# Order of work in three attention stages of a two-block transformer kernel: where weight halves, turns and tiles stand

## The chip, the cores and the metric

The kernel runs on one core of one Trainium2 chip, in one launch. The metric is the device time in microseconds (us), the median over runs. In the kernel and below, PE is TensorE, ACT is ScalarE, DVE is VectorE, POOL is GpSimd and SP is SyncE, which here only issues DMAs.

## The reference, cut to what matters

The input is one sequence of 512 tokens with 1024 features, all in fp32. A first block has two layers; each mixes three branches (latent attention with 4 heads, gated linear attention, retention) and then runs a wide gated feed-forward net. A second block has three more branches: dilated windows, grouped queries, and an attention over 256 memory rows.

```python
# first block, twice
z = rmsnorm(x, attn_norm[l]) @ w_in[l]
y_a = head_rmsnorm(mla_branch(...), mla_out_norm[l])          # causal, 4 heads, 4 blocks of 128 queries
y_b = gla_branch(...)
y_c = retention_branch(...)                                   # head norm, times silu(gate)
x = x + jnp.concatenate([y_a, y_b, y_c], axis=-1) @ w_out[l]
x = x + (jax.nn.silu(causal_dwconv(a)) * bv) @ ffn_w_down[l]
# second block
qb_, kb_ = normed and turned queries (8 heads) and keys (2 heads)
ob = softmax(qb_ @ kb_.T) @ vb_                               # the grouped-query branch
kvm = rms_norm(mem, g_mem) @ w_mem_kv                         # 256 memory rows
om = softmax(mq @ km.T) @ vm
merged = gates[0] * ((oa*silu(ga)) @ w_br_a) + gates[1] * ((ob*silu(gb)) @ w_br_b) + gates[2] * (...)
x = x + rms_norm(merged @ w_out, g_post)
```

## The kernel before, in words

**Products in halves.** Every fp32 matrix is held as a high part and a low part (`w_hi`, `w_lo`; `h_hi`, `h_lo`), and a product is three matmuls: high by high, low by high, high by low (lines 863 to 865, and 1285 to 1287 for the layers' output projection). A "tile" is 128 output rows by 512 tokens and takes 24 matmuls where the inner size is 1024, 12 where it is 512.

**Weights.** They come in chunks of two tiles, into one of two slots of `w_raw`. For each chunk SP issues the load, ACT writes the high part (`high2` in the second block, line 1816; `next_high`, line 1564, in the first), DVE the low part (`split2`, line 2362; `split`, line 1973). SP's load of chunk c waits until chunk c-2 has been split, since both use one slot. PE waits for the split of a chunk before its first tile (`split_ready`). All instructions stand in each engine's queue in the order in which the code emits them, and an engine does not pass a waiting instruction.

**The layers' attention** (`att_pe`, `att_act`, `att_dve`) goes over 16 items, 4 heads for each of 4 query blocks, widest block first. Per item PE makes scores two items ahead, turns the item's probabilities with `ident` (`turn`, line 495, one transposing matmul per 128 keys) and multiplies the turned probabilities of the item before with the values (`values`, line 506). DVE takes the maximum of the scores (line 597) and at the end of every four items writes the normalised output `y_mla` (`norm`, lines 578 and 582). ACT makes the exponentials (line 554) and copies the turned probabilities out of PSUM (line 548). `turn(i)` waits for the exponential of item i and for the copy of item i-1, since there is one turning bank. The first `values` of a block of four waits for `norm` of the block before.

Other work stands between the items by number, in the tables called `fill`: the retention branch (`ret_pairs`, `ret_turn`, `ret_update`, `ret_out`), the turning of the mixed result `y` (`turn_y`, line 1277), its high part on ACT (`high_y`, line 1727) and low part on DVE (`low_y`, line 2236), the norms of `y_mla` (`mla_squares`, `mla_factor`, `mla_scaled`), and the first output tiles (`out_linear` and `out_part`, lines 1285 to 1287). `turn_y(0)` writes bank 7, from which DVE has to have read the retention's sums first (`lin_update`, lines 2097 and 2101, tile `um_r`).

**The grouped-query branch** (`pair_pe`, `pair_act`, `pair_dve`) goes over 16 pairs of heads. For pair p PE runs `turn(p,0)`, slot 3p, `scores(p+1)`, `turn(p,1)`, slot 3p+1, `values(p)`, slot 3p+2. The lines are 639 (turn), 626 (scores) and 650 (values). ACT runs copy(p,0) (line 697), slot 3p, copy(p,1), the two exponentials of pair p+1 (line 690), slot 3p+1, slot 3p+2. DVE takes the maxima of pair p (line 744) and then its slots 3p-2, 3p-1 and 3p. `turn(p,1)` on PE waits for copy(p,0) on ACT. In the slots stand the tiles of the first merge (`merge_tile` on PE, `merge_copy` on ACT, `merge` on DVE): 16 tiles k = 0 to 15, of which those with k % 4 below 2 are gates (24 matmuls, cut into parts 0 and 1) and the others branch outputs (12 matmuls). Which tile has which slot comes from `SLOT_B`. After an odd tile ACT's `copy2` writes the high part of a later chunk at once, and DVE splits that chunk.

**The memory's turns** follow the branch. PE makes two gate tiles (`chunk2(C2_GB)`), turns the 256 memory rows with 16 transposing matmuls (line 1476), two for each of eight blocks, where block k > 3 waits for ACT's copy of block k-4 (`mem_t`, line 1889), then makes the other two gate tiles (`sgate_b`). ACT squares the memory (line 792), DVE adds the squares (line 2491), PE sums them over partitions (`norm_stat`, line 798).

Of the kernel before, what the change touches and what calls it, by code (L numbers as in the profile page):

```python
# [124 lines left out]
def build(nc, A, out, PER):  # L125
# [9 lines left out]
    with ctx:  # L135
# [213 lines left out]
        C2_MA = C2_GA + 2  # L349
# [572 lines left out]
        UNITS_B = [(k, part) for k in range(2, 16) for part in ((0, 1) if k % 4 < 2 else (None,))]  # L922
        SLOTS_B = sorted([0] + [3 * p + 1 for p in range(PAIRS)] + [3 * p + 2 for p in (3, 7, 11)])
# [3 lines left out]
        def slots(*pairs_):  # L927
            out = defaultdict(list)
            for k, f in pairs_:
                out[k].append(f)  # L930
            return out

# [163 lines left out]
        def _(pe):  # L1096
# [35 lines left out]
            with pe.Fori(0, DEPTH) as l:  # L1132
# [156 lines left out]
                def out_linear(m, *js):  # L1289
# [7 lines left out]
                    0: partial(ret_pairs, 0), 1: partial(ret_pairs, 2), 3: ret_turn, 4: ret_update, 6: partial(ret_out, 0),  # L1297
                    5: partial(turn_y, 0), 7: lambda: (ret_out(1), turn_y(1)), 8: partial(out_linear, 0, 0), 9: partial(out_linear, 0, 1),
                    10: lambda: (turn_y(2), turn_y(3)), 12: partial(out_linear, 0, 2), 13: partial(out_linear, 1, 0, 1),
                    14: partial(out_linear, 1, 2), 15: lambda: (out_linear(0, 3), out_linear(1, 3))},  # L1300
# [6 lines left out]
                for j in range(4):  # L1307
                    out_part(3, j)
                for j in range(4, KD):
                    turn_y(j)  # L1310
                for first in (0, 2):
# [92 lines left out]
            def merge_tile(c0, k, first, part=None):  # L1404
# [5 lines left out]
                else:  # L1410
                    tile2(2 * c0 + k, K=4, hi=gt_hi, lo=gt_lo)
# [66 lines left out]
            tile2(2 * C2_GB + 2)  # L1478
            pe.wait_ge(sem("mem_t"), upto(pe, "mem_t", 8))
            norm_stat(pe, 3, mem_sq[:, 0], STAT_BANK)  # L1480
            tile2(2 * C2_GB + 3)
# [69 lines left out]
        def _(act):  # L1551
# [48 lines left out]
            with act.Fori(0, DEPTH) as l:  # L1600
# [129 lines left out]
                def mla_factor(q):  # L1730
# [10 lines left out]
                    5: partial(high_y, 0), 6: lambda: (lin_copy(1, o_sb_r, (0, 3), (0,)), mla_factor(0)),  # L1741
                    7: lambda: (lin_copy(1, o_sb_r, (0, 3), (1,)), ret_squares(), high_y(1)), 8: partial(lin_factor, 1),
# [61 lines left out]
            def copy2(tile, dst, **kw):  # L1804
                copy_tile(tile, bank2[tile], dst, **kw)
                if tile % 2:
                    high2(tile // 2 + 2)
# [11 lines left out]
            def merge_copy(b, c0, k):  # L1819

                half, n = k % 2, 2 * (k // 4) + k % 2
                if k % 4 < 2:
                    if k > 3:
                        act.wait_ge(sem("merged"), upto(act, "merged", 8 * b + n - 1))
                    copy2(2 * c0 + k, gate_br[:, half], func=ACT.Tanh, scale=0.5, bias=g2[:, 32 + 8 * b + n:33 + 8 * b + n])
                else:
                    copy2(2 * c0 + k, y_br[:, half], scale=0.5)
# [786 lines left out]
```

## Time and profile before

| what | value |
|---|---|
| median of three runs | 2001.36 us (2000.72, 2001.36, 2004.78) |
| the profiled execution | 2004.78 us, its span 2002.6 us |
| PE busy | 1966.5 us, 98% |
| DVE busy | 1150.6 us, 57% |
| ACT busy | 826.2 us, 41% |
| mean granted TensorE clock | 0.995 |
| HBM traffic | 85 GB/s over the span |

The page's chain that ended last lies on PE for 88% of the span. The two layers' attention stands at about 166 to 230 us and 769 to 833 us, the grouped-query branch at 1580 to 1701 us, the memory's turns at 1712 to 1717 us. Some 36 us of the span are left in which PE is not busy, the start of the program (15 us until its inputs are there) among them.

### The profile page before, as it was taken

Reading aid. Unit: us, or ns where it says so; the run is one execution under the profiler, and the core shown is the slowest. Engines: PE = TensorE matmul, PEld = TensorE weight load, DVE = VectorE, ACT = ScalarE, POOL = GpSimd, SP = SyncE. Lnnn points to the kernel's source line nnn. Section 1 sums busy time; section 2 is a strip of 40 time slices with the busy share of each in tenths; the row PEclk is TensorE's granted clock in tenths of the full one; section 3 lists DMA queues with packets and bytes.
Section 4 is the critical chain, followed back from the end, with each engine's and each line's share of the span. In section 5 each row is a group of like instructions: output and inputs, shape, how many; then the busy total and the mean of one; then the engine's idle time right before and its main releaser. Section 6 shows DMA issues by size and latency. Waiting matters only on the chain.

```text
span 2002.6 us, 29029 instructions
## 1 busy us (share of the span) xinstructions
PE 1966.5 (98%) x10962; PEld 1613.9 (81%) x10962; DVE 1150.6 (57%) x1382; ACT 826.2 (41%) x1211; POOL 25.9 (1%) x52
## 2 busy tenths in 40 slices
PE   7999999999999999999999999999999999999998
PEld 5897788888887897788888888987777766798888
DVE  6866765655445866766555445846664633443435
ACT  5445443333223345443333222334445555554444
POOL 2001000000000001000000000000000000000000
PEclk8999999999999999999999999999999999999999
DMA  6213133332224223133332223523332212232222
GB/s 192 75 47 105 43 105 105 84 105 85 94 95 120 69 55 106 43 105 96 93 104 85 95 95 80 183 73 99 89 110 68 63 53 64 84 115 76 92 87 85
DMA packets 239916, 181.26 MB, mean 91 GB/s; under 512 B 12842, under 2 KB 232232, under 8 KB 239422
## 3 DMA queue, kind: packets, MB, share of 16 engines
q1 hardware_dynamic: 237856, 177.37, 29.6%
q0 software_dynamic: 1520, 1.17, 0.3%
q10 hardware_dynamic: 430, 1.23, 0.3%
q8 instruction: 72, 1.18, 0.2%
q14 instruction: 38, 0.31, 0.1%
HBM read 168.21 MB, written 2.10 MB: 85 GB/s over the span
## 4 chain that ended last, share of the span: by engine, by line
PE 88%; DVE 6%; issue 2%; ACT 2%; DMA 1%; SPq 0%; DVEq 0%; ACTq 0%
PE ps L863 24%; PE ps L865 23%; PE ps L864 23%; PE ps L626 2%; PE ps L650 2%; PE ps L639 2%; DVE amat L2087 2%; PE ps L1285 1%; PE ps L1286 1%; PE ps L1287 1%; PE ps L506 1%; PE ps L475 1%; DMA w_raw<-in_w_in_dram 1%; PE ps L1169 1%; PE ps L495 1%
## 5 line engine op out<-in xcount | busy, mean ns | idle before, releaser
L863 PE MATMUL ps<-h_hi,w_hi 128*128 128x512 f32 x1376 | 553.8, 402 | 2.3 <-ACT qk L1557 2.0
L865 PE MATMUL ps<-h_hi,w_lo 128*128 128x512 f32 x1376 | 541.0, 393 | 0.0
L864 PE MATMUL ps<-h_lo,w_hi 128*128 128x512 f32 x1376 | 537.1, 390 | 0.0
L1973 DVE TENSOR_TENSOR w_lo<-w_raw,w_hi 128x2048 fp32r<-128x2048 f32 (+3 forms) x110 | 227.2, 2065 | 225.5 <-ACT w_hi L1564 218.0
L863 PEld LDWEIGHTS ps<-h_hi,w_hi 128*128 128x128 f32 x1376 | 259.4, 189 | 61.0 <-issue 7.4
L865 PEld LDWEIGHTS ps<-h_hi,w_lo 128*128 128x128 f32 x1376 | 259.2, 188 | 59.6
L864 PEld LDWEIGHTS ps<-h_lo,w_hi 128*128 128x128 f32 x1376 | 259.5, 189 | 56.0 <-issue 1.9
L1564 ACT ACTIVATE w_hi<-w_raw 128x2048 fp32r<-128x2048 f32 (+3 forms) x108 | 186.8, 1729 | 232.4 <-PE ps L865 211.9
L2362 DVE TENSOR_TENSOR w_lo<-w_raw,w_hi 128x1024 fp32r<-128x1024 f32 (+1 forms) x118 | 126.5, 1113 | 167.4 <-ACT w_hi L1816 166.7
L863 PE MATMUL ps<-w_hi,h_hi 128*128 128x256 f32 x544 | 152.4, 280 | 0.3 <-DVE h_lo L837 0.2
L864 PE MATMUL ps<-w_lo,h_hi 128*128 128x256 f32 x544 | 150.7, 277 | 0.0
L865 PE MATMUL ps<-w_hi,h_lo 128*128 128x256 f32 x544 | 150.7, 277 | 0.0
L863 PE MATMUL ps<-hid_hi,w_hi 128*128 128x512 f32 x352 | 138.7, 394 | 0.0
L865 PE MATMUL ps<-hid_hi,w_lo 128*128 128x512 f32 x352 | 138.0, 392 | 0.0
L864 PE MATMUL ps<-hid_lo,w_hi 128*128 128x512 f32 x352 | 136.6, 388 | 0.0
L1816 ACT ACTIVATE w_hi<-w_raw 128x1024 fp32r<-128x1024 f32 (+1 forms) x118 | 108.3, 965 | 4.1 <-issue 2.2
L863 PEld LDWEIGHTS ps<-w_hi,h_hi 128*128 128x128 f32 x544 | 102.3, 188 | 1.9 <-DVE h_lo L837 0.7
L1765 ACT ACTIVATE rms_a<-a_pad,g 128x512 f32<-128x512 f32 x44 | 35.9, 817 | 162.5 <-DVE a_pad L2298 162.5
L864 PEld LDWEIGHTS ps<-w_lo,h_hi 128*128 128x128 f32 x544 | 102.3, 188 | 0.1
L865 PEld LDWEIGHTS ps<-w_hi,h_lo 128*128 128x128 f32 x544 | 102.2, 188 | 0.0
L2303 DVE SCALAR_TENSOR_TENSOR rms_a<-a_pad,g,rms_a 128x512 f32<-128x512 f32 x88 | 66.2, 752 | 58.3 <-ACT rms_a L1765 51.7
L865 PEld LDWEIGHTS ps<-hid_hi,w_lo 128*128 128x128 f32 x352 | 66.1, 188 | 15.5
(390 smaller groups left out, 2767.6 us busy)
## 6 DMA issues: line engine op xcount, KB each, us to landing
w_raw<-in_ffn_w_up_dram SPq DMA_DIRECT2D x88, 512.0 KB, 4.6
w_raw<-in_w_in_dram SPq DMA_DIRECT2D x41, 1024.0 KB, 5.3
w_raw<-in_w_in_dram SPq DMA_DIRECT2D x32, 512.0 KB, 5.2
w_raw<-in_ffn_w_down_dram SPq DMA_DIRECT2D x32, 512.0 KB, 4.0
w_raw<-in_w_out_dram SPq DMA_DIRECT2D x12, 1024.0 KB, 5.6
w_raw<-in_ffn_w_down_dram SPq DMA_DIRECT2D x16, 384.0 KB, 3.4
swapped<-qk SPq DMA_DIRECT2D x96, 64.0 KB, 2.0
w_raw<-in_w_mem_kv_dram SPq DMA_DIRECT2D x4, 1024.0 KB, 5.8
```

Source lines behind the costliest of these rows:

```text
L626: ins = pe.matmul(ps[:, b, c:c + n], lhs, rhs, start=True, stop=True)
L639: ins = pe.transpose(ps[:, T_BANK + c // 512, c % 512:c % 512 + P], probs[:, e, c:c + P], ident)
L650: ins = pe.matmul(ps[64 * e:64 * e + 64, O_BANK, r * P:r * P + P], pairs[p].pv[e][k], probs_t[:, e, k * P:k * P + P], start=(k == 0), stop ...
L863: pe.matmul(dst, lh, rh, start=first and j == 0, stop=False)
L864: pe.matmul(dst, lh, rl, start=False, stop=False)
L865: ins = pe.matmul(dst, ll, rh, start=False, stop=last and j == len(order) - 1)
L1564: act.activation(w_hi[:, slot, 0:n], w_raw[:, slot, 0:n], ACT.Copy).then_inc(sem("w_high"), 1)
L1816: act.activation(w_hi[:, slot, q * n:q * n + n], w_raw[:, slot, q * n:q * n + n], ACT.Copy).then_inc(sem("w_high"), 1)
L1973: dve.tensor_tensor(w_lo[:, slot, 0:n], w_raw[:, slot, 0:n], w_hi[:, slot, 0:n].bitcast(F32), ALU.subtract).then_inc(sem("w_split"), 1)
L2087: dve.copy_predicated(amat[:].rearrange("p h t n -> p (h t) n"), levels[:, lv:lv + 1, :].to_broadcast([P, 4 * NT, P]), ps[:, MAIN:MAIN + 4 ...
L2303: dve.scalar_tensor_tensor(conv[:], a_pad[:, s, w:w + S], g[:, bass.ds(G_CONVW + w * KF + f, 1)], conv[:], ALU.mult, ALU.add).then_inc(sem ...
L2362: ins = dve.tensor_tensor(w_lo[:, slot, q * n:q * n + n], w_raw[:, slot, q * n:q * n + n], w_hi[:, slot, q * n:q * n + n].bitcast(F32), AL ...
```

## The change

It changes no computation and no shape; instructions change their place in the queues.

- Layers' attention, PE: `turn_y(0)` goes from item 5 to item 6, `out_linear(0, 1)` from item 9 to item 8, `turn_y(2)` and `turn_y(3)` from item 10 to item 11, `out_linear(1, 0, 1)` from 13 to 12; after the attention `out_part(3, 3)` goes behind the turns of `y_mla`. ACT: `high_y(0)` goes to item 6, `high_y(1)` ahead of `ret_squares`. DVE: `mla_squares(0)` goes ahead of `low_y(0)`, `split(17)` from item 13 to item 7, `low_y(1)` from item 8 to item 7, `mla_squares(2)` from item 12 to item 13.
- Grouped-query branch: tile 15 is cut into two parts, the first in the new slot 45. The high parts behind the odd tiles 3 to 13 leave `copy2` and go to the next pair's slot 3(p+1) on ACT, behind copy(p+1,0); their splits go to slot 3(p+1)+1 on DVE, one pair later than before for most of them.
- Memory's turns: the high part of chunk `C2_GB + 2` goes behind the eight copies `mem_t`; on PE the sum over the squares goes behind the tile `2 * C2_GB + 3`.

```diff
-        UNITS_B = [(k, part) for k in range(2, 16) for part in ((0, 1) if k % 4 < 2 else (None,))]
-        SLOTS_B = sorted([0] + [3 * p + 1 for p in range(PAIRS)] + [3 * p + 2 for p in (3, 7, 11)])
+        UNITS_B = [(k, part) for k in range(2, 16) for part in ((0, 1) if k % 4 < 2 or k == 15 else (None,))]
+        SLOTS_B = sorted([0] + [3 * p + 1 for p in range(PAIRS)] + [3 * p + 2 for p in (3, 7, 11)] + [3 * PAIRS - 3])
...
+        def odd_b():
+            return [(i, k) for i, (k, part) in SLOT_B.items() if k % 2 and part != 0 and k < 15]
...
-                    0: partial(ret_pairs, 0), 1: partial(ret_pairs, 2), 3: ret_turn, 4: ret_update, 6: partial(ret_out, 0),
-                    5: partial(turn_y, 0), 7: lambda: (ret_out(1), turn_y(1)), 8: partial(out_linear, 0, 0), 9: partial(out_linear, 0, 1),
-                    10: lambda: (turn_y(2), turn_y(3)), 12: partial(out_linear, 0, 2), 13: partial(out_linear, 1, 0, 1),
-                    14: partial(out_linear, 1, 2), 15: lambda: (out_linear(0, 3), out_linear(1, 3))},
+                    0: partial(ret_pairs, 0), 1: partial(ret_pairs, 2), 3: ret_turn, 4: ret_update, 6: lambda: (turn_y(0), ret_out(0)),
+                    7: lambda: (ret_out(1), turn_y(1)), 8: partial(out_linear, 0, 0, 1), 11: lambda: (turn_y(2), turn_y(3)),
+                    12: lambda: (out_linear(0, 2), out_linear(1, 0, 1)), 14: partial(out_linear, 1, 2), 15: lambda: (out_linear(0, 3), out_linear(1, 3))},
...
-                for j in range(4):
+                for j in range(3):
                     out_part(3, j)
                 for j in range(4, KD):
                     turn_y(j)
+                out_part(3, 3)
...
             tile2(2 * C2_GB + 2)
+            tile2(2 * C2_GB + 3)
             pe.wait_ge(sem("mem_t"), upto(pe, "mem_t", 8))
             norm_stat(pe, 3, mem_sq[:, 0], STAT_BANK)
-            tile2(2 * C2_GB + 3)
...
-                    5: partial(high_y, 0), 6: lambda: (lin_copy(1, o_sb_r, (0, 3), (0,)), mla_factor(0)),
-                    7: lambda: (lin_copy(1, o_sb_r, (0, 3), (1,)), ret_squares(), high_y(1)), 8: partial(lin_factor, 1),
+                    6: lambda: (high_y(0), lin_copy(1, o_sb_r, (0, 3), (0,)), mla_factor(0)),
+                    7: lambda: (lin_copy(1, o_sb_r, (0, 3), (1,)), high_y(1), ret_squares()), 8: partial(lin_factor, 1),
...
-            def copy2(tile, dst, **kw):
+            def copy2(tile, dst, split=True, **kw):
                 copy_tile(tile, bank2[tile], dst, **kw)
-                if tile % 2:
+                if tile % 2 and split:
                     high2(tile // 2 + 2)
...
-                     fill=slots(*[(i, partial(merge_copy, 0, C2_MA, k)) for i, (k, part) in SLOT_B.items() if part != 0]))
+                     fill=slots(*[(i, partial(merge_copy, 0, C2_MA, k, k == 15)) for i, (k, part) in SLOT_B.items() if part != 0],
+                                *[(i // 3 * 3 + 3, partial(high2, C2_MA + k // 2 + 2)) for i, k in odd_b()]))
...
-                copy2(2 * C2_GB + k, sgates[1][:, k], func=ACT.Silu)
+                copy2(2 * C2_GB + k, sgates[1][:, k], False, func=ACT.Silu)
...
             act.wait_ge(sem("mem_turned"), upto(act, "mem_turned", KD))
+            high2(C2_GB + 2)
             norm_sq(act, tiles_of(mem_t), tiles_of(mem_sq))
...
-                    4: partial(lin_update, 1, um_r, (3, 7), lambda t: ret_c), 5: lambda: (low_y(0), mla_squares(0)),
-                    6: partial(mla_scaled, 0), 7: partial(lin_squares, 1, o_sb_r, um_r), 8: partial(low_y, 1),
+                    4: partial(lin_update, 1, um_r, (3, 7), lambda t: ret_c), 5: lambda: (mla_squares(0), low_y(0)),
+                    6: partial(mla_scaled, 0), 7: lambda: (split(17), low_y(1), lin_squares(1, o_sb_r, um_r)),
                     9: partial(lin_gated, 1, o_sb_r, sig_r, LIN["ret"]["gate"]), 10: partial(mla_squares, 1),
-                    11: lambda: (low_y(2), low_y(3)), 12: lambda: (mla_scaled(1), mla_squares(2)), 13: partial(split, 17),
+                    11: lambda: (low_y(2), low_y(3)), 12: partial(mla_scaled, 1), 13: partial(mla_squares, 2),
...
-                     fill=slots((0, partial(split2, C2_MA + 2)), *[(i, partial(merge, 0, C2_MA, k)) for i, (k, part) in SLOT_B.items() if k % 4 > 1],
-                                *[(i, partial(split2, C2_MA + k // 2 + 2)) for i, (k, part) in SLOT_B.items() if k % 2 and part != 0]))
+                     fill=slots((0, partial(split2, C2_MA + 2)), *[(i, partial(merge, 0, C2_MA, k)) for i, (k, part) in SLOT_B.items() if k % 4 > 1 and part != 0],
+                                *[(i // 3 * 3 + 4, partial(split2, C2_MA + k // 2 + 2)) for i, k in odd_b()],
+                                (3 * PAIRS - 2, partial(split2, C2_MA + 9))))
```

Three places in the queues, before and after. The changed file has a few lines more, so the same operation has a line number 3 to 6 higher there.

First place: PE in a layer's attention, items 5 and 6, before. L506 is `values`, L1277 `turn_y(0)`, L475, L481 and L487 are scores, L495 is `turn`.

```order
L506 MATMUL ps<-v_mla,prob_t 128x128 x3
L1277 MATMUL ps<-cm,tm 128x128 x4
L475 MATMUL ps<-kn,qn 128x256
L495 MATMUL ps<-cm,prob 128x128 x3
L475 MATMUL ps<-kn,qn 128x256
L481 MATMUL ps<-kr,qr 128x256 x2
L487 MATMUL ps<-cm 128x128 x2
L506 MATMUL ps<-v_mla,prob_t 128x128 x3
L1169 MATMUL ps<-tm,amat_r 128x64 x4
L1166 MATMUL ps<-um_r,qk_r 128x256
```

After:

```order
L506 MATMUL ps<-v_mla,prob_t 128x128 x3
L475 MATMUL ps<-kn,qn 128x256
L495 MATMUL ps<-cm,prob 128x128 x3
L475 MATMUL ps<-kn,qn 128x256
L481 MATMUL ps<-kr,qr 128x256 x2
L487 MATMUL ps<-cm 128x128 x2
L506 MATMUL ps<-v_mla,prob_t 128x128 x3
L1280 MATMUL ps<-cm,tm 128x128 x4
L1172 MATMUL ps<-tm,amat_r 128x64 x4
L1169 MATMUL ps<-um_r,qk_r 128x256
```

The turn of `y` (four matmuls) stood ahead of the scores of items 8 and 9 and of turn 6. It now stands behind them, ahead of the retention's output (L1172 and L1169 there).

Second place: ACT in the grouped-query branch, from the copy of tile 5 to that of tile 6, before. `prob_bt` (L697) are the copies of turned probabilities, two per pair, `prob_b` the exponentials, `w_hi` (L1816) the high part of a chunk in two halves.

```order
L1557 ACTIVATE gate_br<-ps,g 128x512
L1816 ACTIVATE w_hi<-w_raw 128x1024 x2
L697 ACTIVATE prob_bt<-ps 128x512 x2
L690 ACTIVATE prob_b,stats<-ps,stats 128x512 x2
L1557 ACTIVATE y_br<-ps 128x512
```

After:

```order
L1560 ACTIVATE gate_br<-ps,g 128x512
L697 ACTIVATE prob_bt<-ps 128x512
L1819 ACTIVATE w_hi<-w_raw 128x1024 x2
L697 ACTIVATE prob_bt<-ps 128x512
L690 ACTIVATE prob_b,stats<-ps,stats 128x512 x2
L1560 ACTIVATE y_br<-ps 128x512
```

The high part stood between the gate's copy and both copies of pair 4; it now stands between the two copies.

Third place: ACT at the memory's turns, from the branch's last copy `norm_bt` on, before. `sgate_b` are the gate tiles, `mem_t` the eight copies that PE's turns wait for, `mem_sq` the squares.

```order
L704 ACTIVATE norm_bt<-ps 128x512
L1881 ACT_TABLE_LOAD
L1557 ACTIVATE sgate_b<-ps 128x512 x2
L1816 ACTIVATE w_hi<-w_raw 128x1024 x2
L1889 ACTIVATE mem_t<-ps 128x256 x8
L792 ACTIVATE mem_sq<-mem_t 128x256 x8
```

After:

```order
L704 ACTIVATE norm_bt<-ps 128x512
L1885 ACT_TABLE_LOAD
L1560 ACTIVATE sgate_b<-ps 128x512 x2
L1893 ACTIVATE mem_t<-ps 128x256 x8
L1819 ACTIVATE w_hi<-w_raw 128x1024 x2
L792 ACTIVATE mem_sq<-mem_t 128x256 x8
```

The high part (2 x 1024 columns) changed places with the eight copies.

## Rows read from the trace of the kernel before

**Rows 1.** The page, its parts 1 and 6

```profile
PE 1966.5 (98%) x10962; PEld 1613.9 (81%) x10962; DVE 1150.6 (57%) x1382; ACT 826.2 (41%) x1211; POOL 25.9 (1%) x52
...
w_raw<-in_w_in_dram SPq DMA_DIRECT2D x41, 1024.0 KB, 5.3
```

**Rows 2.** Waits of PE, whole span: total us, times, longest

```profile
PE ps L639 <- ACT prob_bt L697: 4.4, 4, 2.0
...
PE ps L1476 <- ACT mem_t L1889: 2.2, 1, 2.2
...
PE ps L1277 <- DVE um_r L2097: 2.1, 2, 1.0
...
PE ps L1285 <- DVE y_lo L2236: 1.8, 4, 0.6
PE ps L495 <- ACT prob_t L548: 1.6, 2, 0.8
PE ps L506 <- DVE y_mla L582: 1.6, 4, 0.6
...
PE ps L798 <- DVE mem_sq L2491: 0.3, 1, 0.3
```

**Rows 3.** Timeline: start, us, operation [idle before]; PE, first layer

```profile
192.18 0.63 PE L1277 MATMUL ps<-cm,tm 128*128 128x128 f32 x4 [1.03 <-DVE um_r L2097]
...
193.08 0.49 PE L495 MATMUL ps<-cm,prob 128*128 128x128 f32 x3
```

**Rows 4.** Timeline, ACT, first layer

```profile
191.32 0.49 ACT L548 ACTIVATE prob_t<-ps 128x384 f32<-128x384 f32 x1
```

**Rows 5.** Timeline, DVE, first layer

```profile
203.58 1.22 DVE L2117 TENSOR_REDUCE stats<-um_r 128x16 f32<-128x1024 f32 x1 [2.86 <-ACT um_r L1630]
...
219.03 2.29 DVE L1973 TENSOR_TENSOR w_lo<-w_raw,w_hi 128x2048 fp32r<-128x2048 f32 x1
```

**Rows 6.** Timeline, ACT, grouped-query branch, pair 4

```profile
1617.77 2.00 ACT L1816 ACTIVATE w_hi<-w_raw 128x1024 fp32r<-128x1024 f32 x2
1619.68 0.58 ACT L697 ACTIVATE prob_bt<-ps 128x512 f32<-128x512 f32 x1
```

**Rows 7.** Timeline, PE, grouped-query branch

```profile
1617.30 1.13 PE L626 MATMUL ps<-k_b,q_b 64*128 64x512 f32 x4
1620.40 0.63 PE L639 MATMUL ps<-cm,prob_b 128*128 128x128 f32 x4 [1.97 <-ACT prob_bt L697]
...
1626.92 1.13 PE L626 MATMUL ps<-k_b,q_b 64*128 64x512 f32 x4
1627.98 0.66 PE L639 MATMUL ps<-cm,prob_b 128*128 128x128 f32 x4
```

**Rows 8.** Timeline, PE, the last pair

```profile
1696.25 0.63 PE L639 MATMUL ps<-cm,prob_b 128*128 128x128 f32 x4 [0.84 <-ACT prob_bt L697]
```

**Rows 9.** Windows: length, busy (x) per engine, granted clock, DMA, GB/s

```profile
190.00:193.00 3.00, 1.97 (x16) 1.78 (x15) 2.83 (x5) 1.31 (x4) 0.00 (x0) 1.00 0.15 50
1621.00:1625.00 4.00, 4.00 (x13) 3.08 (x11) 1.61 (x3) 2.15 (x5) 0.00 (x0) 0.57 0.55 179
1717.00:1721.00 4.00, 4.00 (x12) 3.10 (x12) 0.00 (x0) 3.71 (x10) 0.00 (x0) 0.58 0.79 261
```

**Rows 10.** Timeline, ACT, the memory's turns

```profile
1712.98 2.00 ACT L1816 ACTIVATE w_hi<-w_raw 128x1024 fp32r<-128x1024 f32 x2
1714.89 3.28 ACT L1889 ACTIVATE mem_t<-ps 128x256 f32<-128x256 f32 x8
```

**Rows 11.** Timeline, PE, the memory's turns

```profile
1715.30 1.69 PE L1476 MATMUL ps<-cm,mem_in 128*128 128x128 f32 x8 [2.18 <-ACT mem_t L1889]
```

**Rows 12.** Timeline, DVE, grouped-query branch

```profile
1618.96 2.36 DVE L2362 TENSOR_TENSOR w_lo<-w_raw,w_hi 128x1024 fp32r<-128x1024 f32 x2 [3.27 <-ACT w_hi L1816]
```

**Rows 13.** Timeline, SP, loads; the high part that uses it

```profile
1621.35 0.37 SPq L972 DMA_DIRECT2D w_raw<-in_w_in_dram  x1
...
1653.50 2.00 ACT L1816 ACTIVATE w_hi<-w_raw 128x1024 fp32r<-128x1024 f32 x2
```

More of the change, by code:

```diff
@@ L1410, in merge_tile @@
                 else:
-                    tile2(2 * c0 + k, K=4, hi=gt_hi, lo=gt_lo)
+                    tile2(2 * c0 + k, K=4, hi=gt_hi, lo=gt_lo, part=part)
             split_ready(0)
@@ L1817, in high2, with merge_copy @@
                                        ACT.Copy).then_inc(sem("w_high"), 1)
-            def merge_copy(b, c0, k):
+            def merge_copy(b, c0, k, split=True):
                 half, n = k % 2, 2 * (k // 4) + k % 2
@@ L1824, in merge_copy @@
                         act.wait_ge(sem("merged"), upto(act, "merged", 8 * b + n - 1))
-                    copy2(2 * c0 + k, gate_br[:, half], func=ACT.Tanh, scale=0.5, bias=g2[:, 32 + 8 * b + n:33 + 8 * b + n])
+                    copy2(2 * c0 + k, gate_br[:, half], split, func=ACT.Tanh, scale=0.5, bias=g2[:, 32 + 8 * b + n:33 + 8 * b + n])
                 else:
-                    copy2(2 * c0 + k, y_br[:, half], scale=0.5)
+                    copy2(2 * c0 + k, y_br[:, half], split, scale=0.5)
             def branch_parts(first):
```

## The prediction

> **What bounds the kernel now.** I read the page first, then PE's waits, then the timelines around each wait, and last the clock by windows. The page says that PE is busy for 98% of the span [rows 1], and that one load of a 1 MB chunk lands 5.3 us after its issue [rows 1]. So time can be won only where PE stands still or runs at the lower clock. PE's waits are few and have names [rows 2]. In the two layers' attention they are 2.1 us (`turn_y(0)` waiting for DVE's `um_r`), 1.8 us (output tiles waiting for `y_lo`, 4 times), 1.6 us (turns waiting for ACT's copy) and 1.6 us (values waiting for `y_mla`): 7.1 us for both layers, in 12 waits. In the grouped-query branch they are 4 waits for ACT's `prob_bt`, 4.4 us, the longest 2.0. At the memory's turns they are 2.2 us for `mem_t` and 0.3 us for the squares. All 14.0 us lie where the change moves instructions.
>
> Two of these waits cost twice. After the 1.97 us wait [rows 7] and the 2.18 us wait [rows 11] the granted clock was 0.57 from 1621 to 1625 us and 0.58 from 1717 to 1721 us; around the 1.03 us wait of the layer it stayed at 1.00 [rows 9]. [...] In 4 us at 0.57 PE loses 4.0 x 0.43 = 1.7 us; at 0.58 again 1.7 us. These 3.4 us stand in no row of waits, since the matmuls only get longer.
>
> **Layers' attention, twice.** In the idle time before a wait's end PE also loses the overlap between one operation's shown end and the next one's start: without a wait the next starts before the end (1626.92 + 1.13 = 1628.05 against 1627.98, 0.07 us [rows 7]). I take 0.1 for each of the 12 waits: 7.1 + 1.2 = 8.3 us for both layers.
> - `turn_y(0)` behind the scores: PE waited for `um_r` until 192.18 [rows 3]. Now one score and turn 6, which came at 193.08, are next. It needs ACT's copy of item 5, over at 191.32 + 0.49 = 191.81 [rows 4]. So the wait doesn't vanish, it becomes a shorter one: turn 6 at about 191.85 is 1.2 us earlier, and `turn_y(0)`, about half of the 0.9 us between 192.18 and 193.08 (the other half is the score), returns 0.45 us of it further down. Gain 0.75 of 1.1.
> - `split(17)`, 2.29 us on DVE at 219.03 [rows 5], stood ahead of the last normalising and squares. At item 7 it lies in the 2.86 us in which DVE waits for the squares of the retention's output [rows 5]. `low_y(1)` comes right behind it, a pair of items earlier than before, so the wait of the second output tile for `y_lo` goes. `y_mla` of the second and third block comes ahead of the values that need it, because the split or `low_y(2)` no longer stands in front.
> - What is late next: turn 10 waits for the copy of item 9, behind the factor of the retention's norm on ACT; I get 0.5 us by going through ACT's and DVE's queues with the shown durations. Turn 14 waits for the copy of item 13: 0.25 us, where copy and turn have only two short operations between them.
> - `out_part(3, 3)`, three matmuls behind the 16 turns, covers the last 0.26 us wait for `y_lo`.
> Per layer that leaves 0.4 + 0.5 + 0.25, about 1.1 of 4.15, hence a gain of 3.0 to 3.5; I take 3.3, 6.6 us for both. The bounds: all waits go, 8.3; or the new waits eat half, 4.
>
> **Grouped-query branch.** The high part of 2.00 us stood on ACT ahead of copy(4,0), which ran at 1619.68 for 0.58 us [rows 6], and PE's `turn(4,1)` came at 1620.40 instead of 1.06 us after the scores (1626.92 to 1627.98), at 1618.36 [rows 7]: 2.0 us. Now the copy starts at 1617.77 and ends at 1618.35: no wait. Pairs 9 and 14 repeat the pattern with less: 4.4 - 1.97 - 0.84 = 1.6 us in two waits [rows 2, 7, 8]. In the last pair no scores stand between the two turns, so PE waits 0.84 us for the copy [rows 8]; half a tile, six matmuls, 1.4 us, now stands there, and the copy takes 0.6. I take 0.8, since two half tiles cost one more start. With 1.7 us of clock the sum is 2.0 + 1.6 + 0.15 (overlap of two waits) + 0.8 + 1.7 = 6.2 us.
> What the high part now delays is copy(p,1). It has a tile of 12 matmuls as cover: PE starts the tile when `turn(p,1)` is done, 2.8 us of work; ACT is free again 2.0 us after copy(p,0) ended, which was 0.6 us before the turn ended, and the second copy takes 0.6. Margin about 1 us. Of the six high parts that move, three are the long form; the three short ones (half as long) have more.
> On DVE the split (2.36 us [rows 12]) now stands behind a merge and ahead of the maxima of pairs 6, 11 and none at 15. The next pair's exponential is then ready some 1 us before PE turns it. If that cover is 0.5 us short it costs 0.5 us twice.
>
> **Memory's turns.** The copies `mem_t` start at 1714.89 because the high part ran from 1712.98 [rows 10]. Without it they start 1.9 us earlier, and PE's fifth turn comes at about 1713.4 instead of 1715.30 [rows 11]: gain 1.9 us, with 0.3 us of the wait left. The last four turns stay at ACT's pace (3.28 / 8 = 0.41 us per copy [rows 10]). The squares' wait, 0.3 us and 0.15 of overlap, goes behind a tile of 24 matmuls. If the clock stays up that is 1.7 us more. Sum 1.9 + 0.4 + 1.7 = 4.0 us. The moved high part still ends before its split is wanted, two tiles later.
>
> [...]
>
> **Sum.** 6.6 + 6.2 + 4.0 = 16.8 us. Against the profiled execution (span 2002.6, 2004.78 with what lies around it) that gives 1988.0. The median of the runs shown is 2001.36, 3.4 us lower. That is just the price of the two slow stretches, so the other two executions may not have had them; then their gain is 13.4 and the time 1988.0 again. If they had them, it is 2001.36 - 16.8 = 1984.6. [...] I take a point between, nearer to the middle: 1986.5 us.
>
> **Rivals.**
> 1. *The waits come back re-timed, the clock falls anyway* (0.2). In a layer DVE has 2.83 of 3 us busy around the wait [rows 9]; it, not the order on PE, may set the pace. Then the layers give 4 instead of 6.6, and with the clock still falling at the memory the sum is 16.8 - 2.6 - 1.7 = 12.5. From 1988.9 (median) to 1992.3 (profiled); I take 1990. For it: DVE's chain there has three operations of 1.2 us and more. Against: the longest of them have idle time ahead of them.
> 2. *The split ahead of the maxima* (0.07). If DVE's later maxima reach PE in each pair whose split is moved, six times up to 2.36 less 1 us, 1.4 us: 8 us back, and the time is 1994. Against: the third of the long ones has no scores behind it, and DVE sits idle 3.27 us before that split now [rows 12].
> 3. *The later splits delay the loads* (0.02), the slower side. SP loads a chunk only after the split two chunks before. Each of six splits comes about one pair later, 6 us. If load and high part stood back to back, PE would wait up to 6 x 6 = 36 us, a net 36 - 17 = 19 slower, 2020. It decides when the room is under 6 us. The trace shows a load issued at 1621.35 and used at 1653.50 [rows 13]; less 5.3 to land [rows 1] that is 27 us of room.
> 4. *Nothing to be seen* (0.04): within 0.2% if another queue takes up the whole gain, which the idle shares of ACT and DVE speak against.
> The forecast itself has 0.67, with its own range 1983.5 to 1989.5.
>
> **Range and chances.** A measurement of this kernel can tell some 0.2% from no change, 4 us. Faster by more needs a gain over 4 us: forecast, rivals 1 and 2 nearly in full, 0.93. Within 0.2%: 0.05. Slower: 0.02. The range runs from all waits gone in every run with slow stretches before (2001.36 - 18.5, less 1) to rival 1 with a little more: 1981.5 to 1992.
>
> **What would show it.** Right: PE's rows for `prob_bt` and `mem_t` gone or under 0.4 us; no wait for `um_r`; `y_mla` and `y_lo` under 0.3 us in sum for each layer, with one new wait for the copy `prob_t` of 0.4 to 0.6 us at turns 6 and 10; a granted clock of 1.00 behind 1620 us and at the memory. The attention of a layer 3 us shorter. Wrong: new rows of PE waiting for `stats`, `prob_b` or `w_lo`, a half-speed stretch behind the memory's turns, or a layer's attention as long as before.

## The result, and the profile after

| what | before | after |
|---|---|---|
| median | 2005.01 us (6 runs, 2000.72 to 2006.02) | 1989.28 us (6 runs, 1987.40 to 1990.87) |
| ratio, 95% interval | | 0.9927 [0.9917, 0.9937] |
| span of the profiled execution | 2002.6 us | 1987.3 us |

The change makes the kernel 0.7% faster, more than the 0.2% that a measurement can tell from nothing. 1986.5 us was forecast, 2.8 us too low but well inside the range; the ratio stands for 14.6 us (12.6 to 16.6) against the forecast's 13.4 to 16.8.

The page of the kernel after, its first lines (before: [rows 1]):

```profile
span 1987.3 us, 29029 instructions
PE 1960.2 (99%) x10962; PEld 1610.8 (81%) x10962; DVE 1150.4 (58%) x1382; ACT 826.0 (42%) x1211; POOL 25.9 (1%) x52
```

The work of ACT and DVE is the same to 0.2 us; only TensorE has less idle and less slow time around it. Its waits in the kernel after, largest first without the kernel's start (line waited for: us in total, times, longest):

```profile
PE ps L495 <- ACT prob_t L548: 2.6, 6, 0.7
...
PE ps L863 <- ACT qk L1560: 2.0, 4, 0.8
PE ps L1184 <- DVE kg L2046: 1.0, 1, 1.0
PE ps L1543 <- DVE h_lo L2520: 0.6, 1, 0.6
PE ps L798 <- DVE sq L2169: 0.4, 2, 0.2
PE ps L495 <- ACT prob_mt L548: 0.4, 1, 0.4
PE ps L626 <- DVE qk L2440: 0.4, 1, 0.4
```

And all of them from 1570 to 1710 us, the grouped-query branch and the memory's turns:

```profile
PE ps L1479 <- ACT mem_t L1893: 0.3, 1, 0.3
```

Against [rows 2] the waits for `um_r`, `y_lo`, `y_mla`, `prob_bt` and `mem_sq` are gone, and the one for `mem_t` fell from 2.2 to 0.3 us. One has grown: turns of the layers wait for ACT's copy `prob_t` 6 times, 2.6 us. These are the three re-timed waits of the forecast, in each layer. Two rows are new, at places that the change leaves alone: `kg`, 1.0 us at the start of the kernel (0.8 in e1, 0.4 in e11, none in the others), and `qk` (L626), 0.4 us at 1434 us (0.3 in e3 and e7, 0.2 in e5, none in the others). PE in the first layer (start, duration, idle before and what ended it; before: [rows 3]):

```profile
192.15 0.52 PE L495 MATMUL ps<-cm,prob 128*128 128x128 f32 x3 [0.37 <-ACT prob_t L548]
...
207.77 0.41 PE L495 MATMUL ps<-cm,prob 128*128 128x128 f32 x2 [0.65 <-ACT prob_t L548]
...
216.23 0.30 PE L495 MATMUL ps<-cm,prob 128*128 128x128 f32 x1 [0.29 <-ACT prob_t L548]
```

0.37, 0.65 and 0.29 us stand where 0.4, 0.5 and 0.25 were forecast for turns 6, 10 and 14; the second layer has the same three. In the grouped-query branch, ACT at pair 4 (before: [rows 6]):

```profile
1612.64 0.60 ACT L697 ACTIVATE prob_bt<-ps 128x512 f32<-128x512 f32 x1
1613.27 2.01 ACT L1819 ACTIVATE w_hi<-w_raw 128x1024 fp32r<-128x1024 f32 x2
1615.18 0.58 ACT L697 ACTIVATE prob_bt<-ps 128x512 f32<-128x512 f32 x1
```

The copy that PE's turn waits for is now ahead of the weight half (the high part), not behind it. PE at the memory's turns (before: [rows 11]):

```profile
1700.78 1.04 PE L1479 MATMUL ps<-cm,mem_in 128*128 128x128 f32 x8
1702.11 1.69 PE L1479 MATMUL ps<-cm,mem_in 128*128 128x128 f32 x8 [0.29 <-ACT mem_t L1893]
...
1714.64 0.59 PE L798 MATMUL ps<-mem_sq,ones 128*128 128x256 f32 x2
```

The statistic of the memory's squares (L798) has no wait left. And the granted clock (third column from the right) behind pair 4's turns and behind the memory's (before: [rows 9]):

```profile
1612.00:1616.00 4.00, 3.92 (x21) 2.57 (x19) 1.38 (x2) 3.90 (x6) 0.00 (x0) 1.00 0.00 0
1616.00:1620.00 4.00, 4.00 (x33) 2.50 (x32) 1.85 (x3) 2.54 (x6) 0.00 (x0) 1.00 0.00 0
1704.00:1708.00 4.00, 4.00 (x20) 3.25 (x19) 1.81 (x2) 3.84 (x8) 0.00 (x0) 1.00 0.00 0
```

Pair 4's second turn starts at 1613.38 here. The clock is 1.00 in all three; before, it was 0.57 and 0.58, and 0.50 in the middle of either stretch (1622 to 1623 and 1718 to 1719 us). The 512-column matmuls start 0.43 us apart in those two stretches, against 0.23 us at 1.00.

**Where the time went, by stage.** The stages below are differences between starts of PE's rows in the profiled executions: *attention* runs from a layer's first scores to the turns of `y_mla`, *output* from there to the statistic of the feed-forward norm, *branch* from the first grouped-query scores to the first memory turn, *memory* from there to the memory attention's first scores. They carry the experiments too. "Slow" counts the 512-column matmuls at the lower clock in the branch and in the memory stage: their rows are 0.60 us and longer, those of almost all others 0.39 or 0.40.

| kernel (us) | attention 1, 2 | output 1, 2 | branch | memory | slow |
|---|---|---|---|---|---|
| before | 60.83, 60.93 | 40.75, 40.74 | 132.04 | 56.99 | 8, 8 |
| after | 57.38, 57.44 | 41.64, 40.90 | 125.86 | 53.04 | 0, 0 |
| e1 layers only | 57.45, 57.41 | 40.91, 40.90 | 130.45 | 56.99 | 0, 7 |
| e2 branch only | 60.83, 60.80 | 40.76, 40.75 | 125.87 | 56.99 | 0, 5 |
| e3 memory only | 60.82, 60.81 | 40.76, 40.75 | 130.46 | 53.03 | 0, 0 |
| e4 one high part | 60.93, 60.83 | 40.74, 40.75 | 129.68 | 57.03 | 0, 0 |
| e5 half of it | 60.83, 60.82 | 40.75, 40.74 | 129.52 | 57.02 | 0, 3 |
| e6 after, high part back | 57.44, 57.44 | 40.90, 40.91 | 125.86 | 54.93 | 0, 0 |
| e7 after, splits later | 57.40, 57.41 | 40.91, 40.90 | 127.77 | 53.02 | 0, 0 |
| e8 after, tile 15 whole | 57.45, 57.46 | 40.90, 40.90 | 126.88 | 53.03 | 0, 0 |
| e9 first turn only | 60.17, 60.15 | 40.75, 40.76 | 132.04 | 57.00 | 8, 7 |
| e10 split 17 only | 59.82, 59.91 | 40.75, 40.75 | 132.05 | 56.81 | 7, 7 |
| e11 after, copy first | 57.24, 57.14 | 40.91, 40.91 | 125.87 | 53.01 | 0, 0 |
| e12 after, statistic back | 57.43, 57.44 | 40.91, 40.91 | 125.86 | 58.67 | 0, 7 |

The stages repeat to 0.1 us in most rows, the median of a kernel only to some 2 us, so verdicts on less than 2 us rest on stages.

From before to after the layers give 3.45 + 3.49, less 0.89 + 0.16 in the output stages (into which `out_part(3, 3)` moved); the branch 6.18; the memory 3.95. Another 0.5 us was lost between second layer and branch, where the new wait of 0.41 us for `qk` stands, and 0.2 us at the start. That is 15.3 us, the difference of the spans. The 0.89 is 0.73 more than in all the other runs that have this edit; for that the forecast has no term, and no wait stands there.

### The profile page after: what moved, and what is told of

Read it like the earlier page. It is cut to its first block, busy times and chain, and to the rows that moved or that the text cites. A ratio compares the mean times of both kernels' runs of the same rounds, so it can differ in the third digit from the quotient of the medians.

```text
span 1987.3 us, 29029 instructions
## 1 busy us (share of the span) xinstructions
PE 1960.2 (99%) x10962; PEld 1610.8 (81%) x10962; DVE 1150.4 (58%) x1382; ACT 826.0 (42%) x1211; POOL 25.9 (1%) x52
## 4 chain that ended last, share of the span: by engine, by line
PE 89%; DVE 6%; issue 2%; DMA 1%; ACT 1%; SPq 0%; DVEq 0%; ACTq 0%
PE ps L863 24%; PE ps L865 23%; PE ps L864 23%; PE ps L626 2%; PE ps L650 2%; PE ps L639 2%; DVE amat L2092 2%; PE ps L1288 1%; PE ps L1290 1%; PE ps L1289 1%; PE ps L506 1%; DMA w_raw<-in_w_in_dram 1%; PE ps L475 1%; PE ps L1172 1%; PE ps L495 1%
```

## The experiments

Ratios are to runs of the kernel before on the same chip.

**e1: the layers' part alone.** Before, with the fills of the layers' attention (PE, ACT and DVE) and `out_part(3, 3)` as in the change:

```diff
-                    0: partial(ret_pairs, 0), 1: partial(ret_pairs, 2), 3: ret_turn, 4: ret_update, 6: partial(ret_out, 0),
-                    5: partial(turn_y, 0), 7: lambda: (ret_out(1), turn_y(1)), 8: partial(out_linear, 0, 0), 9: partial(out_linear, 0, 1),
...
+                    0: partial(ret_pairs, 0), 1: partial(ret_pairs, 2), 3: ret_turn, 4: ret_update, 6: lambda: (turn_y(0), ret_out(0)),
+                    7: lambda: (ret_out(1), turn_y(1)), 8: partial(out_linear, 0, 0, 1), 11: lambda: (turn_y(2), turn_y(3)),
...
```

> Only the layers' part of the change. Theory: each attention saves its waits less three new short ones, 3.3 us per layer (2.8 of it ahead of the turns of y_mla, the rest behind), 6.6 us in all, ratio 0.9967; the grouped-query branch and the memory's turns stay at 132.0 and 57.0 us, with both stretches at the lower clock. Rival (the parts help each other through the loads): under 4 us here and more than the sum in the whole change.

Measured: 1997.22 us, ratio 0.9962 [0.9948, 0.9976]. The attention stages are 3.4 and 3.5 us shorter, the output stages 0.16 longer, 3.3 us net per layer, as forecast. The branch took 130.45 us and not the 132.0 that was expected; e3 shows the same.

**e2: the branch's part alone.** Before, with tile 15 halved, six high parts behind the next pair's first copy, and their splits on DVE one pair later for most of them (not shown):

```diff
-                    copy2(2 * c0 + k, y_br[:, half], scale=0.5)
+                    copy2(2 * c0 + k, y_br[:, half], split, scale=0.5)
...
+                                *[(i // 3 * 3 + 3, partial(high2, C2_MA + k // 2 + 2)) for i, k in odd_b()]))
...
```

> Only the grouped-query branch's part. Theory: its stretch, from the first scores to the first turn of the memory, goes from 132.0 to 125.9 us, 6.2 us, of which 1.7 is the clock; the memory's turns keep their 2.2 us wait and the lower clock behind it, although they come 6 us earlier. Rival (the lower clock belongs to a moment of the run, not to the wait): one of the two slow stretches stays or goes without regard to the wait.

Measured: 1999.35 us, ratio 0.9978 [0.9968, 0.9988]. The branch takes 125.87 us, the whole change's figure, and PE has no wait left in it; the memory's wait of 2.18 us is still there.

**e3: the memory's part alone.** Before, with `high2(C2_GB + 2)` behind the memory's copies and the statistic behind the second gate tile:

```diff
+            tile2(2 * C2_GB + 3)
             pe.wait_ge(sem("mem_t"), upto(pe, "mem_t", 8))
             norm_stat(pe, 3, mem_sq[:, 0], STAT_BANK)
-            tile2(2 * C2_GB + 3)
...
```

> Only the memory's part. Theory: from the first turn of the memory to the memory's attention 57.0 goes to 53.0 us, 4.0 us, of which 1.7 is the clock; clock at 1.00 behind the turns although PE only transposes there. Rival (transposes alone let the clock fall): 2.3 us, and a stretch at half speed behind the turns.

Measured: 1999.49 us, ratio 0.9978 [0.9968, 0.9987]; the memory stage takes 53.03 us. The three parts don't touch each other: their ratios multiply to 0.9918, against 0.9927 for the whole.

This run and e1 also show something that nothing in them changed. PE in e3 at pair 4, and the clock of the stretch behind it:

```profile
1619.02 0.63 PE L639 MATMUL ps<-cm,prob_b 128*128 128x128 f32 x4 [1.97 <-ACT prob_bt L697]
```

```profile
1620.00:1624.00 4.00, 4.00 (x33) 2.97 (x31) 1.92 (x3) 2.49 (x6) 0.00 (x0) 1.00 0.70 227
```

The wait of 1.97 us is there, the same as in before, but the clock doesn't fall, and the branch takes 130.46 us instead of 132.04. In before, e9 and e10, whose branch has the same code, it fell each time, to 0.57 over 4 us. So the lower clock is worth 1.6 us in the branch, and it comes in some executions only: 3 of the 5 profiled here.

**e6: the whole change, the high part back ahead of the memory's copies.**

```diff
-                copy2(2 * C2_GB + k, sgates[1][:, k], False, func=ACT.Silu)
+                copy2(2 * C2_GB + k, sgates[1][:, k], func=ACT.Silu)
...
-            high2(C2_GB + 2)
             norm_sq(act, tiles_of(mem_t), tiles_of(mem_sq))
```

> The whole change, with the high part of the memory's stage back ahead of the eight copies. Theory: the wait of 2.2 us for mem_t is back, now some 11 us earlier in the run than in the kernel before, and so is the stretch at half speed of about 3.4 us: 3.6 us slower than the whole change (the 0.4 us of the squares stays won). Rival (the slow stretch was a matter of the moment): the wait is back and the clock stays up, 1.9 us slower.

Measured: 1989.72 us, ratio 0.9928 [0.9911, 0.9944]. PE's wait is back at full length, and the clock behind it is 1.00:

```profile
1702.17 1.69 PE L1479 MATMUL ps<-cm,mem_in 128*128 128x128 f32 x8 [2.18 <-ACT mem_t L1893]
```

```profile
1704.00:1708.00 4.00, 4.00 (x19) 3.29 (x18) 0.00 (x0) 3.71 (x10) 0.00 (x0) 1.00 0.80 262
```

The stage is 1.9 us longer than in after, not 3.6: the rival held. Yet it is 2.06 us shorter than before, and all that is left of the change in this stage is the place of the statistic, for which the forecast had 0.4 us.

**e4: one high part alone.** Before, with the high part behind tile 5 moved behind the first copy of pair 4 on ACT; DVE's split stays where it was:

```diff
-                     fill=slots(*[(i, partial(merge_copy, 0, C2_MA, k)) for i, (k, part) in SLOT_B.items() if part != 0]))
+                     fill=slots(*[(i, partial(merge_copy, 0, C2_MA, k, k != 5)) for i, (k, part) in SLOT_B.items() if part != 0],
+                                (12, partial(high2, C2_MA + 4))))
...
```

> The kernel before, where only the high part behind tile 5 moves behind the copy of pair 4 on ACT. Theory: PE's turn of pair 4 no longer waits (2.0 us) and the clock behind it stays at 1.00 (1.7 us): 3.7 us, the branch's stretch 128.3 instead of 132.0 us; the other three waits of 0.80, 0.80 and 0.84 us stay. Rival (DVE's split now ends later and takes it back): under 2.5 us, with PE waiting for stats or prob_b.

Measured: 2002.77 us, ratio 0.9997 [0.9987, 1.0007]. PE's wait of 1.97 us is gone, but two smaller ones have come behind it (the rival of the expectation):

```profile
1621.83 0.66 PE L639 MATMUL ps<-cm,prob_b 128*128 128x128 f32 x4 [0.55 <-ACT prob_b L690]
...
1623.99 0.63 PE L639 MATMUL ps<-cm,prob_b 128*128 128x128 f32 x4 [0.45 <-ACT prob_bt L697]
```

DVE in the same stretch shows why:

```profile
1617.94 2.36 DVE L2363 TENSOR_TENSOR w_lo<-w_raw,w_hi 128x1024 fp32r<-128x1024 f32 x2 [3.90 <-ACT w_hi L1816]
1620.21 1.41 DVE L744 TENSOR_REDUCE stats<-ps 128x1 f32<-128x512 f32 x2
```

The split stands ahead of the next pair's maxima and now starts later, because its high part does. So the exponential behind the maxima is late. With the clock up in both, the branch is 0.8 us shorter (129.68 against 130.46), of 2.0 us that the wait lost. In e2, where DVE's splits move too, neither of the two new waits is there; the other 1.2 us are put down to that, but no run moves this one split alone. The last row that matters here is PE's in the memory stage, which this kernel leaves alone:

```profile
1720.34 0.67 PE L798 MATMUL ps<-mem_sq,ones 128*128 128x256 f32 x2 [1.85 <-DVE mem_sq L2492]
```

The clock stayed up here (1.00 from 1712 to 1716 us), PE came to the statistic early, and waited 1.85 us for the squares instead of the 0.26 us of before; the stage is 57.03 us all the same. With 8, 7, 5, 3 and 0 slow matmuls (before, e1, e2, e5, e4) it is 56.99 to 57.03 us each time, and the wait for the squares 0.26, 0.26, 0.44, 0.88 and 1.85 us. The statistic starts 12.26 or 12.27 us after the first memory turn in all five. PE's clock cost nothing in this stage; the chain through ACT and DVE set it. (In e9 the stage is as long; in e10 it is 56.81, the 0.18 us less lie behind the statistic and are unexplained.)

**e12: the whole change, the statistic back ahead of the second gate tile.** If that is so, the high part's move alone is worth nothing, since it now stands ahead of the squares.

```diff
             tile2(2 * C2_GB + 2)
-            tile2(2 * C2_GB + 3)
             pe.wait_ge(sem("mem_t"), upto(pe, "mem_t", 8))
             norm_stat(pe, 3, mem_sq[:, 0], STAT_BANK)
+            tile2(2 * C2_GB + 3)
```

> The whole change, but in the memory part the statistic of the memory's squares stands ahead of the second sigmoid-gate tile again, as in the kernel before; the weight half stays behind the memory's copies. The memory stage (first turn of the memory to the memory attention's first scores) was 56.99 us before, 53.04 with the whole change and 54.93 with the weight half put back. Theory, formed from those runs: the squares' chain on ScalarE and VectorE sets the statistic in the old order, whatever TensorE's clock does, and the weight half now stands in ScalarE's queue between the copies and the squares, so what the turns gain (1.9 us) the squares give back. TensorE's wait for mem_t stays at 0.3 us, its wait for mem_sq grows from 0.26 us to about 3.7 us (1.85 us, as measured at full clock, plus 1.9), and the stage is 57.0 us again, 4.0 longer than with the whole change; time about 1993 us. Rival, the accounting of the prediction: each edit takes away its own wait, so moving the statistic back costs 0.4 us at most and the stage is 53.4 us. Second rival: the squares start when the copies are done as before (VectorE's half covers the weight half), and the stage is 55.1 us.

Measured: 1993.38 us, ratio 0.9949 [0.9935, 0.9962]. ACT's queue, then PE:

```profile
1699.04 3.29 ACT L1893 ACTIVATE mem_t<-ps 128x256 f32<-128x256 f32 x8
1702.37 2.01 ACT L1819 ACTIVATE w_hi<-w_raw 128x1024 fp32r<-128x1024 f32 x2
1704.28 3.54 ACT L792 ACTIVATE mem_sq<-mem_t 128x256 f32<-128x256 f32 x8
```

```profile
1710.41 0.67 PE L798 MATMUL ps<-mem_sq,ones 128*128 128x256 f32 x2 [3.75 <-DVE mem_sq L2497]
```

The theory's wait of 3.7 us is there, and both rivals fall. The stage is even longer than the 57.0 expected, 58.67 us: behind this wait seven matmuls ran slow (clock 0.50 from 1712 to 1714 us), and nothing hides them here (1.6 us, the branch's figure). Without them it would be the 57.0 of before, an estimate, since this kernel was profiled once. So the high part's move without the statistic's gains nothing, and in this execution the stage was 1.7 us longer than before.

**e5: half of the high part ahead of the copy.** Before, with the two halves of the high part behind tile 5 apart, `(11, high2(..., (0,)))` and `(12, high2(..., (1,)))`.

> The kernel before, where the high part behind tile 5 is cut: one half stays ahead of the copy of pair 4, the other goes behind it. Theory (the clock falls after a wait of 2 us and not after one of 1 us): the wait is about 1.0 us, the granted clock stays at 1.00, and the branch's stretch is 129.3 us, 2.7 us less for 1.0 us less wait. Rival (the clock falls wherever PE waits behind a gate tile): 131.0 us, with the half-speed stretch.

Measured: 2002.72 us, ratio 0.9995 [0.9985, 1.0005]. PE's wait is 1.03 us, the clock stays up (1.00 from 1619 to 1623 us) and the branch takes 129.52 us (129.3 expected); but since it also stays up behind 1.97 us in e1 and e3, the run doesn't say that the shorter wait is the reason. The branch is 0.94 us shorter than at full clock with the long wait, about the wait's own 0.94.

**e7: the whole change, five splits one pair later still.**

```diff
-                                *[(i // 3 * 3 + 4, partial(split2, C2_MA + k // 2 + 2)) for i, k in odd_b()],
+                                *[(min(i // 3 * 3 + 7, 43), partial(split2, C2_MA + k // 2 + 2)) for i, k in odd_b()],
```

> The whole change, with five of DVE's six moved splits one pair (6 us) later still. Theory (27 us of room between a chunk's load and its use): no change, branch 125.9 us. Rival (the late splits already sit close to the loads' or the tiles' path): every pair later costs up to 6 us at some of them, 5 to 30 us slower, with PE or ACT waiting for w_lo or w_raw.

Measured: 1989.07 us, ratio 0.9927 [0.9910, 0.9945], the branch 1.9 us longer than in after. PE, then DVE in front of it:

```profile
1624.64 0.50 PE L863 MATMUL ps<-h_hi,w_hi 128*128 128x512 f32 x1 [0.68 <-DVE w_lo L2367]
```

```profile
1621.49 0.69 DVE L2421 SCALAR_TENSOR_TENSOR merged<-gate_br,y_br 128x512 f32<-128x512 f32 x1 [2.63 <-ACT y_br L1560]
1622.22 2.36 DVE L2367 TENSOR_TENSOR w_lo<-w_raw,w_hi 128x1024 fp32r<-128x1024 f32 x2
```

In after this split starts at 1618.84, where the branch begins 2.1 us later; so it is 5.5 us later in e7. There it reaches the tile that needs it: two waits of 0.68 us for `w_lo`. Set beside the same rows in after, the first puts everything behind it off by 0.93 us and the second by another 0.95, which is the 1.9. PE waits for no load there. The theory of no change fails, and so does the rival's 5 to 30 us; the time itself can't tell the two kernels apart. So the forecast's rival 3 looked at the wrong end of the chain: the room before the load is large, that before the tile less than one pair.

**e8: the whole change, tile 15 not halved.**

```diff
-        UNITS_B = [(k, part) for k in range(2, 16) for part in ((0, 1) if k % 4 < 2 or k == 15 else (None,))]
+        UNITS_B = [(k, part) for k in range(2, 16) for part in ((0, 1) if k % 4 < 2 else (None,))]
...
```

> The whole change with tile 15 uncut in its old slot. Theory: PE waits 0.84 us again between the two turns of the last pair, the branch's stretch is 126.7 instead of 125.9 us. Rival (the cut is worth nothing, since a half tile costs a start and the normaliser waits behind it): 125.9 us.

Measured: 1988.90 us, ratio 0.9928 [0.9910, 0.9946]; the branch is 1.0 us longer, and one row of waits is back: 

```profile
PE ps L639 <- ACT prob_bt L697: 0.8, 1, 0.8
```

**e9: only the layers' first turn of `y` (`turn_y(0)`) behind the scores,** on PE, ACT and DVE (`6: lambda: (turn_y(0), ret_out(0))` instead of `5: partial(turn_y, 0)`).

> The kernel before, where only the first turn of y, its high part and the order of its low part move (items 5 to 6). Theory: PE waits 0.4 us for the copy of item 5 instead of 1.03 us for um_r; the stretch from the first scores to the turns of y_mla goes from 60.8 to some 60.1 us, since the later waits for y_mla and y_lo stay. Rival (the later waits take it up): no change, with the wait before item 9 longer.

Measured: 2001.67 us, ratio 0.9994 [0.9984, 1.0003]; the attention stages are 0.7 and 0.8 us shorter, as the forecast's 0.75.

**e10: only split 17 in DVE's idle time** (`7: lambda: (split(17), lin_squares(1, o_sb_r, um_r))` instead of `13: partial(split, 17)`).

> The kernel before, where only DVE's split of the 18th chunk moves from item 13 to item 7 (and the squares of block 2 to item 13). Theory: the 0.81 us wait at turn 15 goes, which is 0.9 us; the split delays the retention's squares by under 0.5 us, which the waits for y_lo and y_mla at items 8 and 9 show: the stretch goes from 60.8 to 60.3 us. Rival (it is free at item 7): 59.9 us.

Measured: 2001.51 us, ratio 0.9989 [0.9980, 0.9999]; the stages are 1.0 us shorter (59.82 and 59.91): the split is free at item 7, as the rival had it. DVE, which had 2.86 us of idle time there in [rows 5]:

```profile
199.97 2.29 DVE L1973 TENSOR_TENSOR w_lo<-w_raw,w_hi 128x2048 fp32r<-128x2048 f32 x1
202.68 1.22 DVE L2117 TENSOR_REDUCE stats<-um_r 128x16 f32<-128x1024 f32 x1 [0.41 <-ACT um_r L1630]
```

The split fits, and 0.41 us of the idle time is left. The other 3.4 - 0.7 - 1.0 = 1.7 us of the attention stage belong, by difference, to the other moves in the layers, which no run takes alone. 0.69 us of them are the three matmuls that now run in the output stage; that stage grows by only 0.16 us, since its wait of 0.26 us for `y_lo` goes, which is worth 0.50 us there.

**e11: the whole change, the copy ahead of the exponential at items 6 and 10 of the layers.**

```diff
+                if i in copy_first:
+                    copy(i - 1)
                 act.wait_ge(sem("nmax"), upto(act, "nmax", base + i + 1))
...
```

> The whole change, and on ACT the copy of item i-1 ahead of the exponential of item i for i = 6 and 10 in the layers. Theory: the two longest waits left in a layer (0.37 and 0.65 us, for prob_t) become waits for the exponential and shrink by some 0.4 us each: a layer's attention is 0.8 us shorter, 1.6 us in all, ratio to the whole change 0.9992. Rival (the exponential itself ends last there, so the order doesn't matter): within 0.3 us.

Measured: 1988.02 us (5 runs, 1986.00 to 1990.32), ratio 0.9920 [0.9907, 0.9934]; the stages are 0.14 and 0.30 us shorter, the rival's figure and not the theory's 0.8. One row says why it isn't more:

```profile
PE ps L495 <- ACT prob L556: 1.5, 4, 0.4
```

The same turns now wait for the exponential, 0.32 and 0.42 us, where they waited 0.37 and 0.65 for the copy. The turn needs both, and ACT does one behind the other. It is the lowest median of all, but its interval covers the changed kernel's.

## Why the prediction came out as it did

**The layers, 6.6 us: right, and nearly so in its steps.** 3.3 us per layer net in e1, the first turn 0.7 (forecast 0.75), the new waits 0.37, 0.65 and 0.29 us for 0.4, 0.5 and 0.25. ACT's and DVE's queues were walked through with the shown durations, not only PE's. The total is closer than the working: by the forecast's own terms it is 4.15 - 1.15 = 3.0 us per layer, and 3.3 was taken without naming the rest. That it came out at 3.3 is in part luck. The term that was too small is the 0.1 us that a wait costs beyond its length: the wait of 0.81 us is worth 1.0 in e10, and the 0.26 us ahead of the output tiles 0.50 (from the turns' start to the tiles', 2.16 us in before and 1.66 in after).

**The branch, 6.2 us: right for the profiled execution (6.18), and its clock term only for some.** Without the slow stretch it is 130.46 - 125.86 = 4.6 us, the forecast's 4.5; the halved last tile gives 1.0 (forecast 0.8). The forecast reckoned with a cover of DVE's split and of the copies that holds; e7 shows that the split could not have gone one pair further.

**The memory, 4.0 us: right as a sum (3.95), but its three terms are not separate prices.** The forecast had 1.9 for the high part, 0.4 for the statistic and 1.7 for the clock. The runs give 1.9 for the high part *once the statistic has moved* (e6), 2.06 for the statistic (e6 against before), and nothing for the clock (e4). The step that failed is reading the slow stretch as a loss of its own. The lower clock in [rows 9] costs PE 1.7 us of the 4; but the next wait behind it, 0.26 us for the squares, means that PE had no one to be late for. The slow matmuls ran in time that would have been a wait. 0.26 + 1.6 is the 1.85 us of e4. So the 4.0 holds also where the clock stays up, for which the forecast had 1.9 + 0.4 = 2.3. In the branch no such wait followed, and the same loss counted in full. In after and e6 no such wait follows in the memory stage either; had the clock fallen there, the 1.6 us would have been lost (an estimate, since it stayed up in both). The edits are also not additive: the high part alone gives nothing, or costs 1.7 us as in e12, and the statistic alone gives 2.06.

**The rivals.** Of rival 1 nothing came. Rival 2 (the split ahead of the maxima) doesn't happen in the kernel after, but e4 shows the mechanism at its real price: of one wait's 2.0 us, 1.2 are lost when only ACT's half moves. Rival 3 has its limit elsewhere (e7).

**The 2.8 us of the point.** The forecast took the lower median, 2001.36, as a sign that the other executions lacked both slow stretches, and chose 1986.5 between its two readings. The later runs of the kernel before have medians of 2003.08 to 2005.01, so the three shown were low. The memory's stretch costs nothing and the branch's 1.6 us, so a difference of 3.4 us can't be the price of the two. The gain is 6.6 + 4.6 + 3.95 = 15.1 us without the branch's slow stretch and 16.7 with it; 1.4 us of it were lost elsewhere in the profiled execution, as the stages say. The first lies in the interval of the ratio (12.6 to 16.6 us), the second at its upper edge. Which part of the runs has the stretch is left open, since only profiled executions show it. There is a hint: of the 67 later runs of the kernel before, 36 have a mean granted clock of 0.997 and the others, 2.1 us longer on average, 0.995 or 0.996; the profiled execution with both stretches had 0.995. But the clock at the kernel's start and end differs between the profiled executions too: 0.72 to 0.86 from 20 to 30 us, 0.89 to 1.00 from 1975 us to the end.

**What stands behind the memory's turns.** PE does nothing but transposes from 1700.78 to 1703.55 us in after, with one wait of 0.29 us among them, and the clock from 1704 to 1708 us was 1.00; e3 has the same wait and 1.00 from 1712 to 1716 us, without a slow matmul. It was 1.00 behind these turns in e7, e8 and e11 too, so the rival of e3, that transposes alone let the clock fall, came in nowhere. With the wait of 2.18 us inside it the stretch is 4.7 us long, and six of eight were followed by the lower clock; whether the transposes on both sides of the wait have a part in it no run separates. In the old order of this stage there were 8, 7, 5, 3 or 0 slow matmuls behind one and the same wait of 2.18 us, in kernels whose instructions are the same there; of each kernel there is one profiled execution.

## What to carry to other kernels

A stretch at the lower clock was a loss here only so far as no wait of PE's stood behind it: it cost 1.6 us in the branch and nothing in the memory stage, where the wait for the squares shrank from 1.85 to 0.26 us. Look at the next wait before you count such a stretch. When a piece of work has halves on two engines (here the high part on ACT and the low part on DVE; with only ACT's moved, 1.2 of 2.0 us were lost), move them together, and put each into idle time that the profile shows ahead of a named wait. Edits on one chain are priced together: walk through the whole chain (copies, weight half, squares, statistic) in the new order, since one edit can be worth nothing, or less, without the other.

## What was not expected of the hardware

Behind a wait of 1.97 us the granted clock fell in three profiled executions (0.50 from 1622 to 1623 us in before, from 1619 to 1620 in e9, from 1620 to 1621 in e10) and stayed at 1.00 behind the same wait, in the same code, in two (1616 to 1620 us in e1, 1620 to 1624 in e3). Behind the memory's wait of 2.18 us it fell in six and stayed up in two (1.00 from 1712 to 1716 us in e4, from 1704 to 1708 in e6). No run here shows what decides it. Where it fell, 3 to 8 matmuls of 512 columns started 0.43 us apart and not 0.23; seven or eight of them cost 1.6 us in the branch. And 512-column matmuls in the first layer's output of the one profiled execution of the kernel after followed each other at 233 ns instead of 229 (226 to 265 us), 0.7 us in that stage, at a granted clock of 1.00 and without a wait; in the output stage of its second layer, and in those of every other run, they did not. Its cause is open.
